# Removal rows in the next stage, gate products behind the last tile, and low-rank products in pairs

## The reference, cut to what matters

```python
p = p + (_token_shift(p) - p) * mu                       # r, w_lo, k, v, a_lo, g_lo
w_log = -softplus(-(w0 + tanh(w_lo) @ w2)) - 0.5         # low rank 1: decay
decay = exp(-exp(w_log))
a = sigmoid(a0 + a_lo @ a2)                              # low rank 2
g = sigmoid(g_lo) @ g2                                   # gate products
kk = heads(k * k_k);  kk = kk / max(norm(kk), 1e-12)     # key norm
k = k * (1.0 + (a - 1.0) * k_a)
y = _rwkv7_scan(rh, heads(decay), kh, vh, -kk, kk * ah)  # -kk: the removal rows
bonus = sum(rh * kh * r_k) * vh
out = (norm(y) * ln_w + ln_b + bonus) * g
```

## Time and profile before

| what | value |
|---|---|
| median of 3 runs | 1596.11 us |
| the profiled execution's own time | 1599.86 us |
| its span, first to last instruction | 1598.1 us |
| PE busy | 1499.9 us, 94% |
| PE weight loads busy | 1268.7 us, 79% |
| DVE, ACT, POOL busy | 708.3 (44%), 641.0 (40%), 411.7 us (26%) |
| mean granted TensorE clock | 0.986 |

### The profile page before, as it was taken

One profiled execution on the slowest core, in us unless ns is written; L12 is line 12 of the kernel. 1 busy time (PEld: TensorE's weight loads), 2 busy tenths in 40 slices (PEclk: granted clock), 3 DMA queues, 4 the chain that ended last, 5 costly groups with the idle time before them and its releaser, 6 DMA issues. The chain is left out here.

```text
span 1598.1 us, 29313 instructions
## 1 busy us (share of the span) xinstructions
PE 1499.9 (94%) x12379; PEld 1268.7 (79%) x12379; DVE 708.3 (44%) x1163; ACT 641.0 (40%) x1026; POOL 411.7 (26%) x107
## 2 busy tenths in 40 slices
PE   4999999898999999999999999978889999999998
PEld 4888897776777878997788877757878888888886
DVE  5344137768754421115544325667555334334002
ACT  5311215766644421107754436432344434434112
POOL 1322221111021233222013322300052444434342
PEclk9999999999999999999999999989999999999999
DMA  9344462243141023138413321000120332221321
GB/s 375 124 159 159 159 185 67 67 106 76 58 159 53 1 106 105 53 104 243 135 53 119 112 79 54 1 13 7 55 92 16 132 105 82 102 105 53 132 100 58
DMA packets 34163, 158.35 MB, mean 99 GB/s; under 512 B 6904, under 2 KB 8440, under 8 KB 19584
## 3 DMA queue, kind: packets, MB, share of 16 engines
q1 hardware_dynamic: 33024, 156.46, 29.6%
q10 hardware_dynamic: 1024, 0.21, 0.1%
HBM read 133.58 MB, written 3.15 MB: 86 GB/s over the span
## 5 line engine op out<-in xcount | busy, mean ns | idle before, releaser
L225 PE MATMUL banks<-ffn_token_parts,ffu_weight_parts 128*128 128x512 f32 (+1 forms) x1056 | 229.7, 380 | 1.2 <-POOL ffu_weight_parts L203 0.9
L225 PEld LDWEIGHTS banks<-ffn_token_parts,ffu_weight_parts 128*128 128x128 f32 x1056 | 191.7, 188 | 38.9 <-POOL ffu_weight_parts L203 1.1
L203 POOL TENSOR_TENSOR even_weight_parts<-weight_chunk,even_weight_parts 128x2048 fp32r<-128x2048 f32 x15 | 70.2, 4681 | 308.7 <-ACT even_weight_parts L197 308.7
L203 POOL TENSOR_TENSOR ffu_weight_parts<-weight_chunk,ffu_weight_parts 128x2048 fp32r<-128x2048 f32 x22 | 101.6, 4618 | 157.3 <-ACT ffu_weight_parts L197 157.3
L225 PE MATMUL banks<-even_token_parts,even_weight_parts 128*128 128x512 f32 (+1 forms) x672 | 124.8, 345 | 0.0
L1008 PE MATMUL banks<-even_token_parts,even_weight_parts 128*128 128x512 f32 (+1 forms) x576 | 122.0, 347 | 0.0
L3332 PE MATMUL banks<-ffd_weight_parts,ffn_f_parts 128*128 128x512 f32 x528 | 120.1, 389 | 1.6 <-PEq L3233 1.6
L225 PEld LDWEIGHTS banks<-even_token_parts,even_weight_parts 128*128 128x128 f32 x672 | 103.5, 188 | 19.5 <-issue 3.8
L225 PE MATMUL banks<-sec_token_parts,sec_weight_parts 128*128 128x512 f32 (+1 forms) x528 | 116.8, 378 | 0.3 <-PEq L300 0.3
L3332 PEld LDWEIGHTS banks<-ffd_weight_parts,ffn_f_parts 128*128 128x128 f32 x528 | 99.0, 188 | 22.5 <-issue 2.0
L3310 DVE SCALAR_TENSOR_TENSOR ffn_conv<-banks,b_ffn_taps,ffn_conv 128x511 f32<-128x511 f32 (+1 forms) x88 | 61.9, 745 | 111.8 <-ACT ffn_conv L3282 108.8
(11 more groups left out here) (461 smaller groups left out, 2673.9 us busy)
## 6 DMA issues: line engine op xcount, KB each, us to landing
weight_chunk<-in_ffn_up SPq DMA_DIRECT2D x22, 1024.0 KB, 4.8
weight_chunk<-in_w_in_even SPq DMA_DIRECT2D x16, 1024.0 KB, 7.1
front_late<-in_w_mod SPq DMA_DIRECT2D x16, 1024.0 KB, 5.1
weight_chunk<-in_w_in SPq DMA_DIRECT2D x13, 1024.0 KB, 4.8
weight_chunk<-in_w_out SPq DMA_DIRECT2D x12, 1024.0 KB, 6.4
weight_chunk<-in_w_in_odd SPq DMA_DIRECT2D x12, 1024.0 KB, 4.9
weight_chunk<-in_ffn_down SPq DMA_DIRECT2D x11, 1024.0 KB, 4.9
front_w<-in_w_mod SPq DMA_DIRECT2D x8, 1024.0 KB, 23.4
```

The source lines that it names most:

```text
L203: (on or self.nc.gpsimd).tensor_tensor(parts[:, 1], self.env.raw[s][:], parts[:, 0].bitcast(F32), ALU.subtract).then_inc(self.lo_done, 1)
L225: m = self.nc.tensor.matmul(o, w, self.env.tok[:, tp, k, a:b], start=k == 0 and n == 0, stop=k == KD - 1 and n == len(PASSES) - 1)
```

## The change

The code moves work between stages and inside the stage; one operation changes engine (the gate's copies go from DVE to ACT), and no arithmetic is added.

```diff
 # stage_second, PE
-                def low_rank(n):
-                    half, f = n // FT, n % FT
...
-                    if n >= 2:
-                        pe.wait_ge(sig_done, n - 1)
-                    rows = slice(half * HD, (half + 1) * HD)
-                    nc.tensor.matmul(
-                        bank(env, LOW_RANK[n % 2]), C2["lora"][rows, f * P : (f + 1) * P], pT[rows, T_LO, :], start=True, stop=True
-                    ).then_inc(low_ready, 1)
+                    for side in range(2):
+                        if f:
+                            pe.wait_ge(sig_done, 2 * f - 1 + side)
+                        rows = slice(side * HD, (side + 1) * HD)
+                        nc.tensor.matmul(
+                            bank(env, LOW_RANK[side]), C2["lora"][rows, f * P : (f + 1) * P], pT[rows, T_LO, :], start=True, stop=True
+                        ).then_inc(low_ready, 1)
...
-                        if r == 3 and k % 2:
-                            low_rank(FT + k // 2)
-                        if r == 9 and k == KD // 2:
+                        if r == 3 and k in (3, 7):
+                            low_rank(2 + k // 4)
+                        if r == 9 and k == 2:
                             key_spread()
+                        if r == RW_TILES - 1 and k == KD // 2:
+                            turn(TX - 1)
                     if r == 2:
                         low_rank(0)
-                        low_rank(1)
...
                     if r == 2:
-                        low_rank(2)
-                        low_rank(3)
-                turn(TX - 1)
+                        low_rank(1)
+                pe.wait_ge(y_done, TX)
+                for f in range(FT):
+                    nc.tensor.matmul(bank(env, 4 + f), C2["g2"][:, f * P : (f + 1) * P], pT[:, T_GL, :], start=True, stop=True)
 # ACT
+                    if r == 3 * TX:
+                        norm(TX - 1)
                     base(rw_job(r))
...
-                    if r and r % 3 == 0:
+                    if r % 3 == 0 and 0 < r < 3 * TX:
                         norm(r // 3 - 1)
 # DVE
                             output_sums(t)
+                            if t:
+                                mixed(t - 1)
                             if r == 8:
                                 for f in range(FT):
                                     unit_keys(f)
                             output(t)
-                            if t:
-                                mixed(t - 1)
...
+                    if r == 11:
+                        decayed_bonus()      # end copy, bT = rate * inv
+                        invert(TX - 1)
                     if r == 12:
-                        decayed_rows()
-                    if r == 13:
-                        removal_rows()
-                mixed(TX - 1)
+                        decayed_keys()       # kT = k_rows * inv
+                        mixed(TX - 1)
 # stage_rwkv_features, ACT
+            for f in range(FT):
+                nc.scalar.copy(W["g"][:, f, :], bank(env, 4 + f)).then_inc(g_out, 1)
 # PE (natural(n) now uses bank n % 4, the bonus products bank 4 + f)
             for n in range(TX):
                 natural(n)
-            for f in range(FT):
-                nc.tensor.matmul(bank(env, f), C2["g2"][:, f * P : (f + 1) * P], pT[:, T_GL, :], start=True, stop=True).then_inc(g_ready, 1)
+            pe.wait_ge(removal, 2)
             for n in range(TX, 2 * TX):
                 natural(n)
 # DVE
+            nc.vector.scalar_tensor_tensor(
+                flat(k)[:, 1 : FT * S], flat(kkn)[:, 1 : FT * S], -1.0, flat(pin)[:, 0 : FT * S - 1], ALU.mult, ALU.mult
+            ).then_inc(removal, 1)
+            dve.wait_ge(removal, 1)
+            nc.vector.tensor_scalar(chunks(k)[:, :, 0:1], chunks(kkn)[:, :, 0:1], -1.0, None, ALU.mult).then_inc(removal, 1)
             nc.vector.tensor_tensor(chunks(ended_b), chunks(bT), ends(), ALU.mult).then_inc(ended, 1)
-            for f in range(FT):
-                dve.wait_ge(g_ready, f + 1)
-                nc.vector.tensor_copy(W["g"][:, f, :], bank(env, f)).then_inc(g_out, 1)
             nc.vector.tensor_tensor(chunks(ended_k), chunks(kT), ends(), ALU.mult).then_inc(ended, 1)
+            nc.vector.tensor_tensor(r, r, pin, ALU.mult)
```

More of the change, by code:

```diff
@@ L1978, in stage_second @@
             sem("norm_out"), sem("inverse_norm"))
-        summed, less_ready, spread_ready, kk_ready, scaled, kt_ready, b_ready, rk_ready, final_step = (
-            sem("summed"), sem("less"), sem("spread"), sem("kk"), sem("scaled_k"), sem("kt"), sem("b_row"), sem("rk"), sem("final_step"))
+        summed, less_ready, spread_ready, kk_ready, scaled, kt_ready, b_ready, rk_ready = (
+            sem("summed"), sem("less"), sem("spread"), sem("kk"), sem("scaled_k"), sem("kt"), sem("b_row"), sem("rk"))
         jobs = [("tile", n) for n in range(CONV)] + [("z", n) for n in range(Z)] + [("tile", n) for n in order]
@@ L2055, in tile, with low_rank @@
                     ring.transposed(c % 2, j % 2, (bank(env, spot(j)),), ((0, S),)).then_inc(tile_ready, 1)
-                def low_rank(n):
-                    half, f = n // FT, n % FT
-                    if n == 0:
+                def low_rank(f):
+                    if f == 0:
                         pe.wait_ge(features_in, 16 * len(feature_consts))
@@ L2311, in _ @@
                         for n in range(2 * FT):
-                            f = n % FT
+                            f, side = divmod(n, 2)
                             act.wait_ge(low_ready, n + 1)
                             nc.scalar.activation(
-                                (rate if n >= FT else inv)[:, f, :], bank(env, LOW_RANK[n % 2]), ACT.Sigmoid,
-                                bias=C2["a0" if n >= FT else "w0"][:, f : f + 1]).then_inc(sig_done, 1)
+                                (inv, rate)[side][:, f, :], bank(env, LOW_RANK[side]), ACT.Sigmoid,
+                                bias=C2[("w0", "a0")[side]][:, f : f + 1]).then_inc(sig_done, 1)
                     if r == 5:
@@ L2408, in running_sum @@
                 def running_sum(f):
-                    dve.wait_ge(sig_done, f + 1)
+                    dve.wait_ge(sig_done, 2 * f + 1)
                     nc.vector.tensor_tensor_scan(inv[:, f, :], C2["reset"][:], inv[:, f, :], 0.0, ALU.mult, ALU.add).then_inc(cum_ready, 1)
@@ L2422, in unit_keys, with decayed_bonus @@
                         by_tile(kkn[:, f, :]), by_tile(k_rows[:, f, :]), C2["k_k"][:, f : f + 1], spread_view(env, 4, f), ALU.mult, ALU.mult).then_inc(kk_ready, 1)
-                def decayed_rows():
+                def decayed_bonus():
                     last = pin.rearrange("p f (c j) -> p f c j", j=RW_CHUNK)[:, :, :, RW_CHUNK - 1]
@@ L2429, in decayed_rows, with decayed_keys @@
                     st.inc(nc.vector.tensor_tensor(bT, rate, inv, ALU.mult))
+                def decayed_keys():
+                    dve.wait_ge(kt_ready, 1)
                     st.inc(nc.vector.tensor_tensor(kT, k_rows, inv, ALU.mult))
[L2432 to L2440, removed]
                 def mixed(t):
@@ L2487, in _ @@
                             output(t)
-                            if t:
-                                mixed(t - 1)
-                    if r and piece == 0:
+                    if piece == 0 and 0 < r < 3 * TX:
                         invert(t - 1)
@@ L2553, in stage_rwkv_features @@
     bT, kT = pT[:, 0:FT, :], pT[:, FT : 2 * FT, :]
-    g_ready, g_out, ended, turned, turned_out, bonus_ready = (
-        sem("g"), sem("g_out"), sem("ended"), sem("turned"), sem("turned_out"), sem("bonus"))
+    g_out, removal, ended, turned, turned_out, bonus_ready = (
+        sem("g_out"), sem("removal"), sem("ended"), sem("turned"), sem("turned_out"), sem("bonus"))
+    pin, kkn, r = W["pin"], W["kkn"], pT[:, T_R : T_R + FT, :]
+    flat = lambda x: x.rearrange("p f t -> p (f t)")
     naturals = [(G_V, v), (G_A, k), (G_B, ended_b), (G_K, ended_k)]
@@ L2562, in _ @@
         def _(act):
+            for f in range(FT):
+                nc.scalar.copy(W["g"][:, f, :], bank(env, 4 + f)).then_inc(g_out, 1)
             for n in range(4 * TX):
                 act.wait_ge(turned, n + 1)
-                nc.scalar.copy(G[:, naturals[n // TX][0], n % TX, :], bank(env, 4 + n % 4)).then_inc(turned_out, 1)
+                nc.scalar.copy(G[:, naturals[n // TX][0], n % TX, :], bank(env, n % 4)).then_inc(turned_out, 1)
         @block.tensor
@@ L2573, in natural @@
                 for f in range(FT):
-                    out, x = bank(env, 4 + n % 4, P, f * P), src[:, f, t * P : (t + 1) * P]
+                    out, x = bank(env, n % 4, P, f * P), src[:, f, t * P : (t + 1) * P]
                     if n < TX:
@@ L2588, in _ @@
                 pe.wait_ge(g_out, f + 1)
-                m = nc.tensor.matmul(bank(env, f), C2["r_k"][:, f, :], rk[:, f, :], start=True, stop=True)
```

(3 more changed lines are left out.)

## The result

The changed kernel takes 1578.03 us (median of 4 runs, 1576.11 to 1579.51), the kernel before 1596.89 (4 runs, 1594.02 to 1598.02): ratio 0.9883, 95% interval 0.9867 to 0.99, so 18.9 us less. Forecast were 1576 and a gain of about 20. In us, the intervals put the gain between 16.0 and 21.2 in the first comparison and between 16.8 and 22.7 in the second.

The account below looks back on a forecast made before the run. PE, busy 94%, sets the pace; savings of 4.2 + 0.8 + 5.6 + 4.4 + 5.6 = 20.6 us take the profiled 1599.86 to 1579.3, carried to the median 1575.5, plus half a microsecond: 1576 us, range 1571 to 1583.

Parts of the forecast that it names:

- Low rank in pairs: Behind tile 2 and in tile 3: low-rank products paired on different partitions run side by side, saving 4.2 us together.
- The reasoning from the key spread: Its 16 products on four partition groups take 1.17 us, like four on one group; so a pair's second product costs nothing.
- The staircase (first rival): In the low-rank pairs: a second product's first half starts only with the first's second half; 1.7 us less gain, 1577.8; 12%.
- `mixed` ahead and the key norm: PE's waits for `mixed` in group 2 and ahead of `scores(3)` go: 0.8 us and 5.6 us saved.
- the spread at step 2: Key spread six products earlier in tile 9, at 1008.6, so keys end before the tile; wait gone with 0.8 us slack.
- End of the stage: Behind tile 13: gate products cover DVE's and ACT's tail, PE ends last, next stage starts at 1051.8, 4.4 us saved.
- The slack that the prediction gave to `turn(3)`: Inside tile 13: `turn(3)` due at 1045.4, after ACT's norm chain ends at 44.0; 1.4 us to spare.
- Features stage: Gate products gone (3.44 us), v products at full clock (2.2 us), removal transposes hidden behind v: 13.7 us, 5.6 saved.
- the clock's, 2.97 + 2.2: Full clock behind the `scores(3)` wait (2.97 us) and in the v products (2.2 us); half a microsecond added for uncertainty.
- no wait stayed: Rival: keys or `turn(3)` late, or the clock falls anyway behind tile 9; costs 3 to 5.6 us, 1579 to 1582; 14%.
- no other engine ended the stretch: Rival: another engine ends the stretch, beyond 1.8 us of cover; the end gives 2 instead of 4.4 us, 1578.4; 5%.
- Low stretches elsewhere: Rival: low-clock stretches shift behind the earlier work, each costing up to 2.97 us; one more 1579, one less 1573; 10%.

Follow-up runs that it names:

- second profile of before: The kernel before the change, unchanged, run and profiled once more: 1596.87 us, its site 127.83 us instead of 129.73.
- second comparison: The changed kernel once more, unedited, 4 runs against 6 of the kernel before: 1577.69 us against 1595.7, ratio 0.9876.
- both late: Changed kernel with the key spread back behind step 4 and `mixed` behind `output` again: site 115.52 us, 6.59 more.

## Why the prediction was right, and where it was off

- **Low rank in pairs:** right, 4.17 against 4.2. The reasoning from the key spread holds. The experiment with both products on one group of partitions splits the gain: 3.3 us from the partitions and 0.8 from fewer inserts, where the prediction had 0.7 for the second part. The staircase (first rival) is out. The clause of TensorE: Matmul & The Clock Gate, Part 3, of the Trainium skill says that matmuls keep program order in start and end. For the starts the trace disagrees: the second product's first half starts at 942.941, ahead of the first product's second half at 943.438. The ends are modelled in the profile and can't test the clause.
- **`mixed` ahead and the key norm:** the size right (0.81 and 5.88 against 0.8 and 5.6), a reason wrong. I gave the 5.6 us to the spread at step 2 together with the order of `mixed`; the runs give all of it to the order. I overlooked that the row products stand ahead of the wait for the keys. Of the 0.24 us more, 0.17 are the two transposes that group 2 has and group 3 has not (7.81 against 7.64 us): I named them but left them in the time at full clock.
- **End of the stage:** right, 4.38 against 4.4. PE ends last: its gate products end at 1037.77, DVE's last instruction at 1035.86, 1.9 us earlier (1.8 in the prediction). The single runs price the gate products as cover (1.5 us), the removal rows (2.7) and the place of `norm(3)` (1.1). The new places of the two decayed rows, and the gate's copies on ACT, were undone in no run; what they are worth alone is open. The slack that the prediction gave to `turn(3)`, 1.4 us, was 1.8 by the last of these runs: ACT's chain began 2.7 us later against PE and left a gap of 0.93. The prediction's "4.5 of its 8 steps" should be 5, which take 3.5 us by a tile's 5.63; its 3.4 is close to that.
- **Features stage:** right, 13.78 against 13.7, 5.56 saved. The removal transposes didn't wait; DVE's two instructions ended at 1040.61, the v products at 1041.72. Of the 5.56 us, 2.12 are the clock, so with the second profile of before the stage saves 5.15.
- **Sum and time:** 20.80 against 20.6 in the profiles, 18.9 and 18.0 in the medians, where 20.1 was forecast. The term most likely off is the clock's, 2.97 + 2.2 in the profile I read. In the second profile of before it is about 1.6 + 1.7, and that alone makes the gain at the site 18.9. I gave it half a microsecond; two would have been nearer. The mean granted clock of the six runs of before in the second comparison says the same: the fastest (1591.93 us) had 0.994, the slowest (1598.45) 0.988. But 20.1 lies inside both intervals of the gain, so the medians by themselves don't show that a term was off; of the 2.0 us between 1576 and 1578.03, 0.8 come from the median of before, 1596.89 with a fourth run. That the forecast is as near as 2 us is in part luck. How often the clock falls, and for how long, over many executions wasn't measured.
- **Rivals:** no wait stayed, no other engine ended the stretch. Low stretches elsewhere did move: behind the site the first profile after has two besides the one at its end (from 1134.9 and 1145.1), the first before has one (from 1156.2).

## What to carry to other kernels

Read an idle gap of PE together with the granted clock behind it: here 2.67 us of waiting cost another 1.6 to 3.1 us through the clock, and 8.2 us another 1.7 to 2.1, so take more than one profile before pricing such a term. Where PE waits for another engine's small step, look first for what merely stands ahead of that step in its queue: one reordered instruction of 0.7 us in each group was worth 6.6 us with the key spread late, about 3.1 of it clock, and 2.1 us with the spread early. When a stage ends on DVE, products that depend on nothing late can fill PE's idle end.

## What the runs showed of the hardware

- Two f32 products of 64 rows and 512 columns on partitions 0 to 63 and 64 to 127 take 1.06 us in all, on the same partitions 1.89. Their two instructions each run as first halves together, then second halves together (942.93 and 942.94, 943.44 and 943.47).
- At the site, idle 0.78, 1.31 and 1.83 us left TensorE's clock at 2.4 GHz; 2.67 us brought 1.2 GHz in all three profiles that had it, 3.00 us didn't, 3.14 did. Elsewhere in the same traces shorter gaps brought it too: idle 1.83 us up to 206.55 in the run with the spread at step 4 and 1.84 us up to 206.96 in the run with pairs on one group of partitions were followed by 1.2 GHz (from 206.8 and 208.2), while 2.16 us at the same place with both late was not. So the length of one gap alone doesn't decide.
